# A bidirectional RWKV recurrence on one core: the products of the two directions woven, on two 64x64 tiles

## The reference, cut to what matters

```
def step(st, inp):
    r_t, w_t, k_t, v_t, a_t, b_t = inp
    sa = jnp.einsum('dbhij,dbhj->dbhi', st, a_t)
    st = st * w_t[..., None, :] + sa[..., None] * b_t[..., None, :] + v_t[..., None] * k_t[..., None, :]
    y = jnp.einsum('dbhij,dbhj->dbhi', st, r_t)
    return st, y
_, ys = lax.scan(step, s0, xs)
y = ys[:, 0] + ys[::-1, 1]
```

## Time and profile before

| | |
|---|---|
| Median of 3 runs | 3411.31 us (3411.3 to 3427.91) |
| Profiled execution, its own time | 3414.5 us |
| Its span, first to last instruction | 3413.2 us |
| PE busy | 3294.1 us, 97% of the span |
| DVE busy, ACT busy | 2287.6 us (67%), 1510.9 us (44%) |
| Mean granted TensorE clock | 0.989 of full |
| Stretch of the eight pairs | 416.9 to about 862 us |

### The profile page before, as it was taken

The page is one execution under the profiler, slowest core; times in us unless marked ns, Lnnn a source line. Parts: engine busy times, 40 slices in busy tenths (PEclk is TensorE's granted clock), DMA queues, the critical chain, the costliest instruction groups (busy, mean ns, idle before and its releaser), DMA issues.

```text
span 3413.2 us, 71697 instructions
## 1 busy us (share of the span) xinstructions
PE 3294.1 (97%) x30194; PEld 3144.8 (92%) x30194; DVE 2287.6 (67%) x2986; ACT 1510.9 (44%) x1811; POOL 75.5 (2%) x154
## 2 busy tenths in 40 slices
PE   8999899999998999899999999989989999999998
PEld 8997898989898859899999999979879899999998
DVE  8776866665587987777755544565655777777545
ACT  5442444444244025544444434454454555445443
POOL 0000100000000000000000000000000000000000
PEclk9999999999999999999999999999999999999999
DMA  8758723232686535577755555534434455555554
GB/s 319 264 198 332 265 86 105 74 113 79 253 322 251 212 137 210 221 282 278 264 186 195 195 194 195 195 118 169 157 115 150 161 195 184 190 191 185 197 193 153
DMA packets 94143, 664.16 MB, mean 195 GB/s; under 512 B 10353, under 2 KB 10993, under 8 KB 15346
## 3 DMA queue, kind: packets, MB, share of 16 engines
q1 hardware_dynamic: 74736, 540.05, 43.8%
q0 software_dynamic: 14400, 104.86, 8.0%
q10 hardware_dynamic: 4802, 16.12, 1.3%
HBM read 654.70 MB, written 6.29 MB: 194 GB/s over the span
## 4 chain that ended last, share of the span: by engine, by line
PE 84%; DVE 10%; DMA 2%; ACT 2%; issue 1%; SPq 0%; DVEq 0%; ACTq 0%
PE ps L462 21%; PE ps L461 21%; PE ps L463 21%; PE ps L433 4%; PE ps L640 2%; PE ps L492 2%; DVE work L1815 2%; PE ps L641 2%; PE ps L642 2%; DMA work<-in_ada 2%; DVE ring_parts L1792 2%; PE ps L708 1%; PE ps L714 1%; PE ps L505 1%; PE ps L699 1%
## 5 line engine op out<-in xcount | busy, mean ns | idle before, releaser
L1792 DVE TENSOR_TENSOR ring_parts<-ring,ring_hi 128x1024 fp32r<-128x1024 f32 x866 | 1042.1, 1224 | 699.8 <-ACT ring_hi L1127 686.5
L1127 ACT ACTIVATE ring_hi<-ring 128x1024 fp32r<-128x1024 f32 x866 | 909.5, 1059 | 1144.4 <-PE ps L463 1089.7
L462 PE MATMUL ps<-h_lo,ring_hi 128*128 128x256 f32 x2624 | 729.4, 278 | 0.0
L461 PE MATMUL ps<-h_hi,ring_hi 128*128 128x256 f32 x2112 | 593.3, 281 | 15.6 <-DVE h_lo L1822 8.5
L463 PE MATMUL ps<-h_hi,ring_parts 128*128 128x256 f32 x2112 | 585.4, 277 | 0.0
L462 PEld LDWEIGHTS ps<-h_lo,ring_hi 128*128 128x128 f32 x2624 | 497.6, 190 | 1.4 <-issue 1.2
L461 PE MATMUL ps<-x_hi,ring_hi 128*128 128x256 f32 x1664 | 466.6, 280 | 10.6 <-DVE x_lo L1822 5.8
L462 PE MATMUL ps<-x_lo,ring_hi 128*128 128x256 f32 x1664 | 462.9, 278 | 0.0
L463 PE MATMUL ps<-x_hi,ring_parts 128*128 128x256 f32 x1664 | 461.1, 277 | 0.0
L461 PEld LDWEIGHTS ps<-h_hi,ring_hi 128*128 128x128 f32 x2112 | 397.3, 188 | 18.3 <-issue 10.0
L463 PEld LDWEIGHTS ps<-h_hi,ring_parts 128*128 128x128 f32 x2112 | 397.1, 188 | 0.0
(11 more groups left out here) (485 smaller groups left out, 5900.4 us busy)
## 6 DMA issues: line engine op xcount, KB each, us to landing
ring<-in_weights SPq DMA_DIRECT2D x511, 1024.0 KB, 4.8
work<-in_ada POOLq DMA_DIRECT2D x96, 1024.0 KB, 7.1
work<-in_c_row POOLq DMA_DIRECT2D x4, 1024.0 KB, 6.0
gate_store<-gate_out ACTq DMA_DIRECT2D x8, 512.0 KB, 3.0
work<-gate_store ACTq DMA_DIRECT2D x2, 2048.0 KB, 17.8
resid<-in_lora ACTq DMA_DIRECT2D x9, 256.0 KB, 2.9
resid<-in_x SPq DMA_DIRECT2D x4, 512.0 KB, 5.9
resid<-in_x ACTq DMA_DIRECT2D x1, 2048.0 KB, 26.9
```

Source lines behind the costliest of these rows:

```text
L461: mm(o, w_hi[:, k, cols], hi(kc), start=(kc == 0 and m % 2 == 0), stop=False, skip_group_check=True)
L462: mm(o, w_hi[:, k, cols], lo(kc), start=False, stop=False, skip_group_check=True)
L1127: A(high_ring(n)[:, 2 * (e % 2) + half, :], ring[:, n % RING, half * (SLOT // 2):(half + 1) * (SLOT // 2)], ACT.Copy)\
L1792: tt(lo, x, high_ring(n)[:, e % 4, :].bitcast(F32), ALU.subtract).then_inc(S("lo_ready"), 1)
```

## The change

It touches the recurrence on three engines and nothing else.

- TensorE: in the doubling, a group holds products of both directions. `each((x_more, 0), (z_of, 1))` goes over chunks and heads and does for each the X product of direction 0 and the Z product of direction 1, one behind the other, both on the same 64x64 tile of the array, because `side(d, h)` is `HALVES[h]` for both directions. The Y products stay in groups of one direction.
- The L products of direction 1 are done twice, into bank 7 (from which its masked copy `LS` is read) and into bank 4 (for Y).
- The first block of gate tiles has 32, not 36; the chunk walk has 4 before `sa` and 4 behind the new state for k = 0, 1, 2 and 4 before `sa` in k = 3. The outputs y of chunk k are done in the next chunk's turn; the `lora` products of the next pair stand in k = 3 before the last of them, and the wait for `pair_done` is left out but for the first pair.
- DVE: slot 2's splits stand between the scaled inputs and the copies of L; slot 3's and the next pair's slot 0 in the chunk walk, between the copies of u and of `sa`; slot 1 stays at the pair's start. L is read by four instructions instead of one and two behind it.
- ACT: slot 3's splits are ahead of the BKT copies; y of a pair is copied in the next pair, behind its sigmoids. The loop is unrolled at its first and last pair.

```diff
-V_STEPS = 8
+V_STEPS = 7
@@ TensorE
+        side = lambda d, h: HALVES[h]
+        def product(out, lhs, rhs, start=False, stop=False):
+            return mm(out, lhs, rhs, start=start, stop=stop, skip_group_check=True)
+        def z_of(d, c, h):
+            return product(PS[HALVES[h], 2 + 3 * d, cols(c)], LS[side(d, h), d, c, :], XY[side(d, h), d, 0, c, :],
+                           start=True, stop=True)
+        def x_more(d, c, h):
+            return product(PS[side(d, h), 3 + 3 * d, cols(c)], XY[HALVES[h], d, 1, c, :], ZS[HALVES[h], d, c, :])
+        def each(*which):
+            for c in range(4):
+                for h in range(2):
+                    ins = [f(d, c, h) for f, d in which]
+            return ins
-            gate_tiles(0, 36, i)
+            gate_tiles(0, 32, i)
-            for e in range(8):
+            for c in range(4):
                 for h, hs in enumerate(HALVES):
-                    ins = mm(PS[hs, 4, e * CH:(e + 1) * CH], AR[hs, e, 0, :], BK[hs, e, 1 - h, :], start=True, stop=True)
+                    product(PS[hs, 4, cols(c)], AR[hs, c, 0, :], BK[hs, c, 1 - h, :], start=True, stop=True)
+                    product(PS[side(1, h), 7, cols(c)], AR[hs, 4 + c, 0, :], BK[hs, 4 + c, 1 - h, :], start=True, stop=True)
+            for c in range(4):
+                for h, hs in enumerate(HALVES):
+                    ins = product(PS[hs, 4, cols(4 + c)], AR[hs, 4 + c, 0, :], BK[hs, 4 + c, 1 - h, :], start=True, stop=True)
...
             for l in range(2, 7):
+                t.wait(S("z_ready"), 1)
+                t.wait(S("x_init" if l == 2 else "xy_ready"), 1)
+                if l > 2:
+                    t.wait(S("yt_ready"), 1)
+                x, z = each((x_more, 0), (z_of, 1))
+                t.give(x, S("xy_mm"))
+                t.give(z, S("z_mm"))
+                if l < 6:
+                    t.give(each((y_more, 0))[0], S("yt_mm"))
+                t.wait(S("z_ready"), 1)
+                if l > 2:
+                    t.wait(S("yt_ready"), 1)
+                if l < 6:
+                    t.wait(S("xy_ready"), 1)
+                    z, x = each((z_of, 0), (x_more, 1))
+                    t.give(z, S("z_mm"))
+                    t.give(x, S("xy_mm"))
+                    t.give(each((y_more, 1))[0], S("yt_mm"))
...
@@ DVE
-            for n in range(2):
-                for half in range(2):
-                    half_split(gates + n, half, i, 4)
+            for half in range(2):
+                half_split(gates + 1, half, i, 4)
-                if hh == 0:
-                    half_split(gates + 2, 0, i, 4)
+            for half in range(2):
+                half_split(gates + 2, half, i, 4)
             t.wait(S("l_mm"), 1)
-            t.give(tt(LS, lp, lm, ALU.mult), S("l_read"))
+            tt(XY[:, 0, 1], lp(4, 0), lvl(1, 1), ALU.mult)
+            tt(XY[:, 1, 1], lp(4, T), lvl(0, 1), ALU.mult)
+            tt(LS[:, 0], lp(4, 0), rows(con("lmask", CH), 4), ALU.mult)
+            t.give(tt(LS[:, 1], lp(7, 0), rows(con("lmask", CH, CH), 4), ALU.mult), S("l_read"))
-                if l < 5:
-                    half_split(gates + 2 + (l - 1) // 2, (l - 1) % 2, i, 4)
+                if k < 2 or more:
+                    half_split(gates + 3 + k // 2, k % 2, i, 4)
```

More of the change, by code:

```diff
@@ L644, in gate_tiles, with lora @@
                     ins.then_inc(S("half_used") if half == 0 else w_used, 1)
-        for i in range(PAIRS):
+        def lora():
             t.wait(S("lw_loaded"), 16)
-            t.wait(S("pair_done"), 1)
             for k in range(4):
@@ L670, in _ @@
                 t.give(ins, S("gram_mm"))
+            t.wait(S("l_read"), 1)
             for d in range(2):
-                if d == 1:
-                    t.wait(S("l_read"), 1)
                 for c in range(4):
@@ L677, in _ @@
                 t.give(ins, S("bkt_mm"))
-            gate_tiles(36, 4, i)
+            gate_tiles(32, 4, i)
             t.wait(S("y_init"), 1)
[L680 to L686, removed]
@@ L718, in _ @@
[L718 to L726, removed]
+            t.wait(S("gram_read"), 1)
@@ new lines, in _ @@
+            for k in range(4):
+                chunk = (k, 3 - k)
+                if k > 0:
+                    t.wait(S("s_ready"), 2)
+                    for h, hs in enumerate(HALVES):
+                        ins = [product(PS[side(d, h), 4 + 3 * d, cols(chunk[d])], AR[hs, 4 * d + chunk[d], 0, :], ST[hs, d, :],
+                                       stop=True) for d in range(2)]
+                    for d in range(2):
+                        t.give(ins[d], S("u_mm"))
+                gate_tiles(36 + 8 * k, 4, i)
+                if k == 0:
+                    t.wait(S("xy_ready"), 2)
+                t.wait(S("u_ready"), 2)
+                for h in range(2):
+                    ins = [product(PS[HALVES[1 - h], 3 + 3 * d, 0:CH], XY[side(d, h), d, 0, chunk[d], :], US[side(d, h), d, :],
+                                   start=True, stop=True) for d in range(2)]
+                for d in range(2):
+                    t.give(ins[d], S("sa_mm"))
@@ L735, in _ @@
+                    y_values(k - 1)
                 if k < 3:
[L736 to L744, removed]
@@ L745, in _ @@
-                if k < 3:
-                    gate_tiles(40 + 8 * k + 2, 2, i)
-                if k > 0:
-                    for d in range(2):
[L749 to L756, removed]
+                    for d in range(2):
+                        e = 4 * d + chunk[d]
+                        t.wait(S("sa_ready"), 1)
@@ L760, in _ @@
                         t.give(ins, S("s_mm"))
[L761 to L769, removed]
+                    gate_tiles(40 + 8 * k, 4, i)
+            if i < PAIRS - 1:
+                lora()
+            t.wait(S("sa_ready"), 2)
+            t.give(y_values(3), S("y_mm"))
         yf = RR_.rearrange("p c t -> p (c t)")
-        t.wait(S("pair_done"), 1)
         t.wait(S("y_stored"), PAIRS)
@@ L1291, in _, with y_store, pair @@
                 half_split(gates + n, half)
-        def pair(i, more):
+        def y_store(i):
+            t.wait(S("y_mm"), 1)
+            act.wait_ge(S("const_loaded"), 32)
+            t.give(A(RR_[:, bass.ds(i, 1), :].rearrange("p a t -> p (a t)"), PS[:, 2, 0:T], ACT.Copy), S("y_stored"))
+        def pair(i, before, more):
             t.wait(S("staged"), 1)
@@ L1301, in pair @@
                                  a["lora2"][bass.ds(i + 1, 1), :, :].rearrange("a p n -> (a p) n")), S("lw_loaded"), 16)
+            if before is not None:
+                y_store(before)
             t.wait(S("vt_ready"), 1)
@@ L1337, in pair @@
             act.dma_start(a["gate_store"][bass.ds(i, 1), :, :].rearrange("a p n -> (a p) n"), G_OUT).then_inc(S("gate_stored"), 16)
[L1338 to L1342, removed]
+        pair(0, None, True)
+        with act.Fori(0, PAIRS - 2) as i:
             t.enter(i, sm)
-            pair(i, True)
-            t.leave(PAIRS - 1)
-        pair(PAIRS - 1, False)
+            pair(i + 1, i, True)
+            t.leave(PAIRS - 2)
+        pair(PAIRS - 1, PAIRS - 2, False)
+        y_store(PAIRS - 1)
         act.wait_ge(S("gate_stored"), 16 * (PAIRS + 1))
@@ L2098, in _ @@
                     t.give(ins, S("v_step"))
-            t.leave(PAIRS)
+        for half in range(2):
+            half_split(gates, half)
+        with v.Fori(0, PAIRS - 1) as i:
+            t.enter(i, sm)
+            pair(i, True)
+            t.leave(PAIRS - 1)
+        pair(PAIRS - 1, False)
         yf, kf, vf = (x.rearrange("p c t -> p (c t)") for x in (RR_, KK_, VV_))
```

78 lines of the change are left out of this document (38 added, 40 removed).

## The result

The changed kernel takes a median of **3447.1 us** (3445.81 to 3453.58, six runs), the kernel before 3412.86 us beside it (3409.26 to 3427.91, six runs): a ratio of **1.009, 95% interval 1.0064 to 1.0116**. Slower, as forecast (3444, range 3426 to 3466). The profiled execution has a span of 3444.5 us at a granted clock of 0.989, the same clock as before.

The account below looks back on a forecast made before the run. TensorE was taken as the bound (PE busy 97%). Terms sum to +4.0 us a pair, 32 for eight, about +1 behind the last: 3447.5 from the profiled 3414.5, 3444 us on the runs' footing, range 3426 to 3466.

Parts of the forecast that it names:

- end of the pair and lora: From u products of k = 3 to the next pair's transposes of v: 5.1 us instead of 4.34, +0.8.
- first gate block: Gate products at the pair's start: four tiles fewer, -1.25, with +0.1 taken for `tilde_ready`.
- L: L products ahead of Gram: eight more per pair at 0.029 us a pass, +0.47.
- wait for `l_read`: TensorE, done with L and Gram at 15.3 us, waits for DVE's reads of L at 16.4: +1.15.
- BKT, start of the doubling: X and Y of both directions before the levels: 2.15 us instead of 2.26, -0.1.
- first Z to the gates of k = 0: Five doubling levels through u: 17.5 us instead of 15.4, a level 3.31 against 3.07, +2.1.
- walk, k = 0: First chunk of the walk: 5.0 us instead of 4.5, waiting for `sa` copies where gate tiles stood, +0.5.
- walk, k = 1 and 2: Middle chunks of the walk: 5.28 us each instead of 5.17, +0.1 each.
- the short queue: Woven groups: one pass waits per tile, second head starts 0.12 us late, +1.9 a pair, 3459 us; chance 0.16.
- tie: First gate block: `tilde_ready` 11.6 us into the pair against TensorE's 11.75, +0.1 taken.
- the rival built on it: Starts in program order: a woven group takes 1.40 instead of 0.93 us, 5.1 a pair, 3485 us; chance 0.06.
- The faster rival: Woven passes overlap four deep: a group takes 0.47 us, 11 save 5.1 a pair, 3402 us; chance 0.03.

Follow-up runs that it names:

- the old order: The changed kernel with Z of both directions first, then X and Y of each direction in turn, unwoven: 3426.53 us, ratio 1.0038, a pair 57.10 us.
- Heads in turn: The changed kernel with woven groups ordered X head 0, X head 1, Z head 0, Z head 1, still two tiles: a pair 59.40 us, total 3451.4 us.
- The later split: The changed kernel with the second half of slot 2 split behind the Gram copies, not ahead of the reads of L: 3439.49 us, ratio 1.0067.
- four tiles: The changed kernel with direction 1's matrices on the other head's half, so a woven group uses four 64x64 tiles: 3415.93 us, ratio 0.9994.
- the run by heads: The changed kernel with every doubling group ordered as all head 0's products, then all head 1's: 3526.79 us, a pair 67.77 us.
- the run with L once: The changed kernel with direction 1's L products done once, into bank 4, masked copy read from there: a pair 59.76 us, total 3474.39 us.

## Why the prediction was right

Step by step, one pair, in us, from the timeline of the middle pair:

| Step | forecast | measured |
|---|---|---|
| end of the pair and lora | +0.8 | +0.74 (651.59 to 656.67, before 4.34) |
| first gate block | -1.15 | -1.27 (596.88 to 608.64) |
| L | +0.47 | +0.51 |
| wait for `l_read` | +1.15 | +0.80 (610.23 to 613.01, before 1.98) |
| BKT, start of the doubling | -0.1 | +0.05 |
| first Z to the gates of k = 0 | +2.1 | +2.67 |
| walk, k = 0 | +0.5 | +0.60 |
| walk, k = 1 and 2 | +0.2 | +0.36 |
| sum | +4.0 | +4.46 |

**The doubling** held in its mechanism and is the largest part: the old order gives back all of it, 2.67 us. Its size was 0.6 too small, and four levels at 3.41 instead of 3.31 make 0.4 of that. Heads in turn brings a level to 3.34, so that 0.07 of the missing 0.10 is the short queue, priced as a rival at 0.12 us a group and worth 0.02 to 0.05. The other 0.03 is in the half with X last: summed as 1.63, because ACT's copy is shorter than DVE's, it takes 1.68 in that run, while the other half, summed as 1.68, takes 1.67. In the change's trace ACT's copy of X and DVE's of Z end together there (625.31 + 0.38 and 625.27 + 0.42).

**The wait for `l_read`** was there, 0.35 below the sum. `tilde_ready` came 608.00 - 596.88 = 11.1 into the pair and not 11.6, so it was no tie: TensorE never waits for it, and the +0.1 fell away as well. From there to the end of line 2088 DVE took 4.96 (608.00 to 612.96) where 4.8 was summed, the two splits 2.56 rather than 2.4. The later split removes the wait and 0.28 behind it.

**L** cost its 0.5 on the timeline, but not by itself: as long as DVE is late, leaving it out is worth nothing (59.76 to 59.79). The prediction lists it and the wait as two costs. Its sum holds, because it took the wait against a TensorE that has done L twice (15.3 us into the pair), but they are one cost: what L takes the wait gives back, so the +0.47 and the +1.15 stand or fall together with DVE's chain.

**The rate of woven passes.** The forecast took it from the order of L751 and L743, and read it as three waiting passes where the rows show four. The first five passes on four tiles show it directly: in program order the first product's second pass stands ahead of the others' first, and three products' first passes start before it. The Trainium skill says otherwise ("TensorE: Matmul & The Clock Gate", section "The mechanism" of Part 3: matmuls are in program order in start and end); here the measured starts decide, and the rival built on it, 3485 us, fell. What the Trainium skill says of tiles ("TensorEngine Tiling (Array Packing)", section "Key Properties": different tiles load and multiply in parallel) agrees: four passes within 0.02 us.

**The faster rival** was refused for the right reason: its condition was four different tiles. With them the woven 32 passes take 0.47 us as it said, but from the first Z to the gates of k = 0 the pair takes 15.34 us (660.15 to 675.49 in that trace), 2.8 less than the change and not the 4.7 of ten halved groups: the rest goes into round trips.

**Footing.** Eight pairs at +4.46 would be 35.7 us; the span has 31.3. The seven intervals sum to +29.5 and not 31.2, in most part because the first differs by 2.85 only (57.79 to 60.64): in the first pair of the changed kernel TensorE goes from Gram to BKT in 1.99 (432.29 to 434.28), without the wait, which is half of it. The last pair, from its lora products to the first product behind the pairs, takes 61.49 us (to 895.31), before 55.64 (to 862.28): 5.9 more, so that 1.4 comes on top of a middle pair where the forecast had 1. That makes 35.4 us for the pairs, against 33 forecast. The code outside, which the change doesn't touch, came out 2.3 us shorter ahead of the pairs and 1.7 behind them. This is the execution's and not the change's: in the traces of the runs, whose code ahead of the pairs is the same, the first lora product stands anywhere from 414.3 to 417.4, and what follows the pairs takes from 2547 to 2576. By the medians the loss is 34.2 us (3412.86 to 3447.1), where the forecast had 33 (3411.3 to 3444). So the mechanism was right; that the total came within 3 us is in part luck, since the pairs lost 2.4 us more than forecast and the code outside gave 4 back. One slip without effect: the 55.9 us for a pair divide the time to the last lora product of the eighth pair; to its first it is 389.7 / 7 = 55.7.

## What to carry to other kernels

Here, weaving two chains helped only where their products lay on different tiles of the array; on the same tile it bought no rate and spread a covered round trip into several bare ones, so count for each group what stands between a result and its first reader. When a step is made faster or left out in front of a wait, first ask who ends the wait: here half a microsecond of TensorE's work more or less was worth nothing while DVE's splits made `l_read` late. Filler work belongs where the trace shows the bare waits (the first Z, the last level, the copies of `sa`), not in one block ahead of them.

## What the runs showed of the hardware

- TensorE starts passes of different 64x64 tiles past three waiting passes of another tile, but not past a fourth of the same one: runs of 2 passes of one tile lose nothing (48 passes in 1.397 us, woven or not), runs of 4 lose 0.02 to 0.05 us in a group of 48, two runs of 8 take 0.74 us between first and last start rather than 0.46.
- One tile takes a pass every 0.058 us in these products (in the run by heads, rows of 2 start 0.12 apart), two tiles one every 0.029, four tiles one every 0.015 (32 passes in 0.47).
- A float32 product's own two passes are not started together even when other tiles are free: on four tiles the first product's start at 659.20 and 659.28, and within the group each tile keeps its 0.058 us a pass.
- Two executions can take the same code at a different pace with the same granted clock of 1.00: passes of 128x256 every 0.116 us in the change's trace and every 0.118 in that of the run with L once.
